# A transformer step with an expert loop: combination inside the next gate products, rows gathered in column tiles, second modulation on the gathered columns

## The reference

```
x = ln_affine(alpha * x + g1 * mix, ln1_g, ln1_b)
h = ln_plain(x) * (1 + sc2) + sh2                # sc2, sh2: one row for context, one for latent tokens
aff = softmax(h @ w_router)                      # 16 experts
gate, idx = top_k(aff.T, cap)                    # 16 of the 128 context tokens, 32 of the 256 latent ones per expert
hid = silu(h[idx] @ w_gate) * (h[idx] @ w_up)    # 1024 -> 2816, per expert
ye = (hid @ w_down) * gate                       # 2816 -> 1024
x = ln_affine(alpha * x + g2 * sum of ye at idx, ln2_g, ln2_b)
```

## Time and profile before

| | |
|---|---|
| median of three runs | 1884.5 us |
| profiled execution | 1881.69 us |
| its span, first to last instruction | 1879.9 us |
| mean granted share of TensorE's clock | 0.939 |
| PE busy | 1751.5 us (93%) |
| VectorE busy | 497.9 us (26%) |
| ScalarE busy | 296.9 us (16%) |
| GpSimd busy | 55.1 us (3%) |
| moved by DMA | 641.58 MB |
| gate and up products (L1096) | 673.3 us |
| down products (L1123) | 328.4 us |

### The profile page before, as it was taken

One profiled execution on the slowest core, in us unless ns is written; L12 is line 12 of the kernel. 1 busy time (PEld: TensorE's weight loads), 2 busy tenths in 40 slices (PEclk: granted clock), 3 DMA queues, 4 the chain that ended last, 5 costly groups with the idle time before them and its releaser, 6 DMA issues.

```text
span 1879.9 us, 19789 instructions
## 1 busy us (share of the span) xinstructions
PE 1751.5 (93%) x8298; PEld 888.3 (47%) x8298; DVE 497.9 (26%) x952; ACT 296.9 (16%) x633; POOL 55.1 (3%) x75
## 2 busy tenths in 40 slices
PE   5999999999979998999989999998999999999996
PEld 2767777778855343333443434333343433334332
DVE  5475647775670101010010101101010110101102
ACT  2443354453330000000000000000000000000000
POOL 2000000010030000000000000000000000000000
PEclk8999999999977999999989898988999999999998
DMA  9683243226565999999999999999999999999993
GB/s 357 226 285 88 96 126 93 84 90 236 223 243 243 423 404 426 430 430 430 434 428 432 429 430 430 429 432 427 416 424 423 414 432 430 429 430 431 431 432 153
DMA packets 60396, 641.58 MB, mean 341 GB/s; under 512 B 6093, under 2 KB 6237, under 8 KB 32701
## 3 DMA queue, kind: packets, MB, share of 16 engines
q1 hardware_dynamic: 56464, 629.96, 81.2%
q0 software_dynamic: 3888, 11.01, 1.8%
HBM read 637.25 MB, written 3.70 MB: 341 GB/s over the span
## 4 chain that ended last, share of the span: by engine, by line
PE 89%; DVE 6%; issue 2%; DMA 2%; ACT 1%; POOL 0%; SPq 0%; DVEq 0%; ACTq 0%
PE banks L1096 36%; PE banks L1123 17%; PE banks L771 16%; PE banks L1043 5%; PE banks L1131 4%; PE banks L769 2%; PE banks L1107 1%; PE banks L725 1%; DVE O L1880 1%; PE banks L786 1%; DMA ring<-in_w_in 1%; PE banks L927 1%; DVE O L1885 1%; PE banks L883 1%; PE banks L948 1%
## 5 line engine op out<-in xcount | busy, mean ns | idle before, releaser
L1096 PE MATMUL banks<-ring,O 128*64 128x512 f32 (+1 forms) x3072 | 673.3, 600 | 10.4 <-DVE O L1868 10.2
L1096 PEld LDWEIGHTS banks<-ring,O 128*64 128x64 f32 x3072 | 222.0, 141 | 451.6 <-issue 450.6
L1123 PE MATMUL banks<-ring,O 128*64 128x512 f32 x1408 | 328.4, 628 | 9.4 <-ACT O L1406 9.4
L1123 PEld LDWEIGHTS banks<-ring,O 128*64 128x64 f32 x1408 | 103.3, 145 | 225.5 <-issue 211.6
L1880 DVE TENSOR_TENSOR O<-O,banks 128x512 f32<-128x512 f32 (+1 forms) x48 | 28.0, 639 | 642.8 <-PE banks L1096 642.8
L771 PE MATMUL banks<-slot_parts,X_parts 128*128 128x512 f32 x672 | 184.8, 405 | 0.0
L771 PEld LDWEIGHTS banks<-slot_parts,X_parts 128*128 128x128 f32 x672 | 122.3, 190 | 39.9 <-issue 11.8
L1885 DVE TENSOR_TENSOR O<-banks,O 128x512 f32<-128x512 f32 x32 | 20.6, 686 | 376.1 <-PE banks L1123 376.1
L1546 DVE TENSOR_TENSOR slot_parts<-ring,slot_parts 128x512 fp32r<-128x512 f32 x168 | 105.2, 685 | 14.9 <-ACT slot_parts L1171 14.2
L1131 PE MATMUL banks<-O 128*128 128x512 f32 x192 | 86.2, 598 | 23.8 <-DVE O L1885 23.8
L1043 PEld LDWEIGHTS banks<-O 128*128 128x128 f32 x768 | 101.9, 216 | 8.5 <-issue 7.2
(11 more groups left out here) (265 smaller groups left out, 1071.2 us busy)
## 6 DMA issues: line engine op xcount, KB each, us to landing
ring<-in_w_exp_up SPq DMA_DIRECT2D x64, 2816.0 KB, 19.3
ring<-in_w_exp_gate SPq DMA_DIRECT2D x64, 2816.0 KB, 23.3
ring<-in_w_exp_down SPq DMA_DIRECT2D x32, 3072.0 KB, 16.8
...
ring<-in_w_mod SPq DMA_DIRECT2D x16, 1024.0 KB, 9.9
ring<-in_w_exp_down SPq DMA_DIRECT2D x16, 1024.0 KB, 22.1
O<-in_w_mod SPq DMA_DIRECT2D x8, 1024.0 KB, 5.2
```

The source lines that it names most:

```text
L1096: x = pe.matmul(banks[64 * w:64 * w + 64, 3 * m + b, 0:(i1 - i0) * P], xeT[:, k, :], w4[:, kk, w, i0 * P:i1 * P], start=(k == 0), stop=(k ...
L1123: x = pe.matmul(banks[64 * w:64 * w + 64, 6 + dc, :], hidT[:, i, 64 * w:64 * w + 64], wd[:, i, w, dc * BANK:(dc + 1) * BANK], start=(i == ...
```

## The change

Five things are changed.

1. The combination of expert e-1 moves into the gate products of expert e: three products after the first quarter, three after the second, into banks 3 to 5; VectorE's six adds move with it, to the start of its part of expert e. The combination of the last expert stays where it was. The slot broadcast of expert 0 moves from behind its gate products to behind their second quarter.
2. The rows of expert e+1 are gathered during expert e, between the turning of the hidden rows and the down products. The selection is now stationary (32 columns) and h2 moving (512 columns); the results of the two tile kinds and the two halves of D go to four groups of 32 partitions of one bank. ScalarE copies them, PE turns them (turn_expert, behind the first down group), and VectorE multiplies by 1 + sc2 and adds sh2 while it writes xeT.
3. h2 holds the plain normalised rows. GpSimd's and VectorE's modulation goes. The router weights are multiplied by 1 + sc2 beforehand (wrg), and 24 products add the share of sh2 to the logits (shift_logits). The order on ScalarE and VectorE around the norms changes with that, and tile 0 is normalised half by VectorE, half by ScalarE. The broadcasts of sc2 and sh2 become six small loads.
4. Feature 22 n + 2 i + w of the weights now lands in hidden column 128 i + n (before: 11 n + i), so gate and up products read elements 22 apart (before: 2) and the turning reads adjacent ones (before: 11 apart).
5. Within the last up quarter PE finishes block after block, VectorE gates each block when it is there, and each block is turned as soon as it is gated.

```diff
+        sc2k, sc2n, sh2k, sh2n = (O3[:, 2944 + 16 * i:2960 + 16 * i].rearrange("p (g k) -> p g k", g=2) for i in range(4))
+        sc2x, sh2x = (O3[:, 3008 + 16 * i:3024 + 16 * i].rearrange("p (i w g) -> p i w g", i=4, w=2) for i in range(2))
+        sc2x_m, sh2x_m = (x.rearrange("p i w g -> p (i w) g") for x in (sc2x, sh2x))
...
-        hid_cols = hid.rearrange("p (n i) -> p i n", i=FT)
-        h2_cols = O4[:].rearrange("p (t k n) -> p t k n", t=T, k=KT)
+        hid_cols = hid.rearrange("p (i n) -> p i n", i=FT)
         def h2_half(t, w):
-            return h2_cols[:, t, 4 * w:4 * w + 4, :]
-
-        def in_columns(row, w):
-            return row.rearrange("p (n k) -> p k n", k=KT)[:, 4 * w:4 * w + 4, :]
-
-        xeT = O3[:, BANK:2 * BANK].rearrange("p (k s) -> p k s", k=KT)
+            return h2[:, t, :].rearrange("p (n w k) -> p n w k", w=2, k=4)[:, :, w, :]
+        xe = O3[:, 0:BANK]
+        xe_cols = xe.rearrange("p (n k) -> p k n", k=4)
+        xeT = O3[:, BANK:2 * BANK].rearrange("p (m s) -> p m s", m=KT)
+        xeT_g = O3[:, BANK:2 * BANK].rearrange("p (m g s) -> p m g s", m=KT, g=2)
...
+            pool.dma_start(l1g, ln1_g.to_broadcast((P, D))).then_inc(bc_loaded, 16)
+            pool.dma_start(l1b, ln1_b.to_broadcast((P, D))).then_inc(bc_loaded, 16)
             for g in range(2):
                 pool.dma_start(g1b[:, g, :], mods[g, 2:3].to_broadcast((P, D))).then_inc(bc_loaded, 16)
-                pool.dma_start(sc2b[:, g, :], mods[g, 4:5].to_broadcast((P, D))).then_inc(bc_loaded, 16)
-            pool.dma_start(l1g, ln1_g.to_broadcast((P, D))).then_inc(bc_loaded, 16)
-            pool.dma_start(wr, w_router[0].rearrange("(p k) e -> p k e", p=P)).then_inc(bc_loaded, 16)
+            pool.dma_start(wr, w_router[0].rearrange("(k p) e -> p k e", p=P)).then_inc(bc_loaded, 16)
             pool.dma_start(iota_r, k_r[1:2].to_broadcast((P, NT))).then_inc(bc_loaded, 16)
-            pool.wait_ge(job_done, J_PB[-1] + 1)
-            for g in range(2):
-                pool.dma_start(sh2b[:, g, :], mods[g, 3:4].to_broadcast((P, D))).then_inc(bc_late, 16)
-            pool.dma_start(l1b, ln1_b.to_broadcast((P, D))).then_inc(bc_late, 16)
-            for n in range(2):
-                for w in range(2):
-                    dst = h2_half(t, w)
-                    pool.tensor_tensor(dst, dst, in_columns(sc2b[:, g, :], w), ALU.mult).then_inc(h2_scaled, 1)
-                    pool.wait_ge(h2_scaled, 2 * n + w + 1)
-                    pool.tensor_tensor(dst, dst, in_columns(sh2b[:, g, :], w), ALU.add).then_inc(h2_ready[n], 1)
+            for q, near, far in ((4, sc2k, sc2n), (3, sh2k, sh2n)):
+                pool.dma_start(near, mods[:, q].rearrange("g (p k) -> p g k", k=KT)).then_inc(bc_loaded, 16)
+                for g in range(2):
+                    pool.dma_start(far[:, g, :], mods[g, q].rearrange("(k p) -> p k", p=P)).then_inc(bc_loaded, 16)
...
+            def shift_logits(n):
+                t = ORDER[n]
+                for k in range(KT):
+                    pe.matmul(banks[:, 4 + t, 0:NE], sh2n[:, min(t, 1), k:k + 1].to_broadcast((P, P)), wr[:, k, :],
+                              start=(k == 0), stop=False)
             def logits(n, b):
                 t = ORDER[n]
                 pe.wait_ge(tb_out[b], F_H2[0] // 2 + n + 1)
                 for k in range(4 * b, 4 * b + 4):
-                    x = pe.matmul(banks[:, 4 + t, 0:NE], h2T[:, k, t * P:(t + 1) * P], wr[:, k, :],
-                                  start=(k == 0), stop=(k == KT - 1))
+                    x = pe.matmul(banks[:, 4 + t, 0:NE], h2T[:, k, t * P:(t + 1) * P], wrg[:, min(t, 1), k, :],
+                                  start=False, stop=(k == KT - 1))
                 if b:
                     x.then_inc(rt_log, 1)
...
-            pe.wait_ge(h2_ready[0], 2)
-            turn_tile(h2, 0)
+            pe.wait_ge(mod2_cols, 2)
+            for n in range(T):
+                shift_logits(n)
+            for n in range(2):
+                pe.wait_ge(h2_norm, n + 1)
+                turn_tile(h2, n)
+                for b in range(2):
+                    logits(n, b)
+            turn_probs(0)
+            pe.wait_ge(h2_first, 1)
+            turn_half(h2, 2, 0)
+            pe.wait_ge(h2_norm, 3)
+            turn_half(h2, 2, 1)
+            turn_probs(1)
             for b in range(2):
-                logits(0, b)
-            for n in (1, 2):
-                for b in range(2):
-                    pe.wait_ge(h2_ready[n], b + 1)
-                    turn_half(h2, n, b)
-                    if n == 2 and b:
-                        turn_probs(0)
-                    logits(n, b)
-            turn_probs(1)
+                logits(2, b)
             turn_probs(2)
...
-            def gather(k, ts):
-
-                s0 = k % 4 * SLOT + (LAT0 if ts[0] else CTX0)
+            def gather(ts):
                 for t in ts:
-                    x = pe.matmul(banks[:, 6 + k // 4, s0:s0 + CAP_L], h2_cols[:, t, k, :], sel[:, t, :],
-                                  start=(t == ts[0]), stop=(t == ts[-1]))
+                    s0 = LAT0 if t else CTX0
+                    for w in range(2):
+                        x = pe.matmul(banks[64 * w + s0:64 * w + s0 + CAP_L, 3, :], sel[:, t, :], h2_half(t, w),
+                                      start=(t < 2), stop=(t != 1))
                 return x
+            def turn_expert(n):
+                pe.wait_ge(xe_cp, n)
+                for i in range(4):
+                    x = pe.transpose(banks[:, 4, i * P:(i + 1) * P], xe_cols[:, i, :], ident)
+                x.then_inc(xet_done, 1)
...
-            for k in range(KT):
-                gather(k, (1, 2))
+            gather((1, 2))
...
-            for k in range(KT):
-                x = gather(k, (0,))
-            x.then_inc(xet_done, 1)
+            gather((0,)).then_inc(xe_done, 1)
+            turn_expert(1)
...
+            def combine(e, ns):
+                for n in ns:
+                    t, dc = divmod(n, 2)
+                    if n >= 3:
+                        pe.wait_ge(acc_done, e * 6 + (6 + n - 2))
+                    pe.matmul(banks[:, 3 + n % 3, :], selT[:, t * P:(t + 1) * P], yrow[:, dc * BANK:(dc + 1) * BANK],
+                              start=True, stop=True).then_inc(comb_done, 1)
+            def block_products(m, q, kk, b):
+                w4 = reg(((4 * m + q) % 6) * QUARTER, QUARTER).rearrange("p (k n i w) -> p k w i n", k=2, i=FT, w=2)
+                k = 2 * q + kk
+                i0, i1 = FCH[b]
+                for w in range(2):
+                    x = pe.matmul(banks[64 * w:64 * w + 64, 3 * m + b, 0:(i1 - i0) * P].rearrange("p (i n) -> p i n", n=P),
+                                  xeT[:, 2 * (k % 4) + k // 4, :], w4[:, kk, w, i0:i1, :], start=(k == 0), stop=(k == KT - 1))
+                return x
             def expert(e, first=False, last=False):
-                pe.wait_ge(xet_cp, 2 * e + 2)
+                pe.wait_ge(xet_cp, e + 1)
+                for q in range(4):
+                    pe.wait_ge(land_g[q], e * 16 + 16)
+                    for kk in range(2):
+                        for b in range(len(FCH)):
+                            x = block_products(0, q, kk, b)
+                    x.then_inc(gate_used, 1)
+                    if first:
+                        if q == 1:
+                            broadcast_slots()
+                    elif q == 0:
+                        pe.wait_ge(selT_ready, e)
+                        pe.wait_ge(y_cp, e * 2)
+                        combine(e - 1, range(3))
+                    elif q == 1:
+                        combine(e - 1, range(3, 6))
+                if first:
+                    pe.wait_ge(rt_cols, 2)
                 pe.wait_ge(acc_done, e * 6 + 6)
-
-                for m, (land, used) in enumerate(((land_g, gate_used), (land_u, up_used))):
-                    for q in range(4):
-                        pe.wait_ge(land[q], e * 16 + 16)
-                        w4 = reg(((4 * m + q) % 6) * QUARTER, QUARTER).rearrange("p (k m w) -> p k w m", k=2, w=2)
-                        for kk in range(2):
-                            k = 2 * q + kk
-                            for b, (i0, i1) in enumerate(FCH):
-                                for w in range(2):
-                                    x = pe.matmul(banks[64 * w:64 * w + 64, 3 * m + b, 0:(i1 - i0) * P],
-                                                  xeT[:, k, :],
-                                                  w4[:, kk, w, i0 * P:i1 * P], start=(k == 0), stop=(k == KT - 1))
-                        x.then_inc(used, 1)
-                    if first and m == 0:
-                        broadcast_slots()
-                        pe.wait_ge(rt_cols, 2)
-
-                pe.wait_ge(hid_done, e * 3 + 3)
+                for q in range(3):
+                    pe.wait_ge(land_u[q], e * 16 + 16)
+                    for kk in range(2):
```

(66 more changed lines are left out.)

96 lines of the change are left out of this document (44 added, 52 removed).

## The result

The changed kernel takes 2712.16 us (median of four runs, 2709.92 to 2714.87), the kernel before 1882.76 in the same comparison: ratio 1.438, 95% interval 1.429 to 1.448. The forecast was 1865, the range 1854 to 1880, and the rival that came true, (a), had 0.20 and a price of 2383 at its high end. The measured time lies beyond even that.

What follows compares the result with a forecast made beforehand. DMA and PE were taken as level, with DMA the bound after the change at 80.4 us per expert. Start -1, queue -9 and end -6.5 sum to -16.5; 1881.7 - 16.5 = 1865 us, range 1854 to 1880, leaving out (a).

Steps and rivals of the forecast that it cites:

- (a): Rival, every gate and up product: the wide step slows them, PE bounds the loop; up to 2383 us; chance 0.20.
- The weights read with a wide step: Gate and up products reading 22 elements apart: expected to cost nothing up to 15% on 41.4 us per expert.
- the low end: Gate and up products: wide step costs nothing, as 0.61 ns per element hides under 0.87 ns per column.
- The high end: Gate and up products: 1.70 ns per element, none hidden, 41.4 becoming 80.9 us; 111.8 per expert, 2383 us in all.
- The decision point of rival (a): Gate and up products: from 49.5 us for both, an expert takes PE more than the 80.4 us of transfers.
- PE in the loop: Expert loop: PE's work falls to 72.3 us per expert, gather 2.6 of it, against 80.4 us of transfers.
- The stretch before the loop: Norms, router and first gather before expert 0: sum -1 us, first gate product at 575, first maximum search at 556.2.
- The shift products: PE after the last output product: 48 records, 5.3 us at full clock or 10.1 at half; 5.3 taken.
- rival (b): Before the loop: shift products at half clock (+4.8) or gathers not abreast (+5); 1870 to 1875 us; chance 0.12.
- rival (c): Before the loop: shorter chain, VectorE no longer slowed beside GpSimd or clock staying high; 1858 us; chance 0.20.
- VectorE's wait for ScalarE: Before the loop: VectorE waits some 8 us for ScalarE's deviation of the second tile, until 541.6 instead of 533.3.
- The queue and the end: Loads at 430 GB/s, last landing 1264.4 us after first gate product: -9; products end 4.7 behind it: -6.5.

Runs made afterwards that it cites:

- experiment 4: Kernel of experiment 3 with the eight gate and up quarters read at steps 1, 2, 3, 4, 6, 8, 11, 22; not the layer; 2182.76 us.
- experiment 3: The full change but with the old feature order (weights 2 apart, turning 11 apart, waiting for all three blocks): 1868.88 us, ratio 0.990; repeated, 1865.24 us, ratio 0.992.
- experiments 7: Kernel of experiment 4 with two-dimensional patterns at steps 2 and 11, steps 12, 16, 32, and other groupings at 22; not the layer; 2387.07 us.
- 8: Kernel of experiment 4 with the eight quarters read at steps 14, 18, 20, 24, 26, 28, 30 and 44; not the layer; 2459.59 us.
- 9b: Kernel of experiment 3 with ScalarE's square roots ahead of tile 0's copies and VectorE's maxima behind tile 2's second norm: 1859.38 us, ratio 0.988.
- 9c: Kernel of 9b with VectorE summing the shift beforehand (3 products for 24) and tile 0's copies ahead of tile 2's square root: 1856.81 us, ratio 0.987.
- experiment 9a: Kernel of experiment 3 with each expert's combination back behind its down products, in six banks, adds behind the scaling: 1868.82 us, ratio 0.991.

## Why the prediction was wrong, and where it was right

**The weights read with a wide step: wrong.** I took the low end, nothing, "as 0.61 hides under 0.87", with up to 15% on it; it was 150%. The 0.61 was the difference of two stationary loads, as if a fetch were an addition to the product's pace. The curve of experiment 4 fits a pace of its own, of which the slower counts: 0.86 ns per column for the product, 1.75 for a fetch that serves one column. The row that I set aside had it: 218 ns for 128 elements 11 apart is 1.70 each, and products 11 apart measured 1.75 in experiment 4. The 3% at step 2, which I held against the rival, is no evidence for wide steps: there the fetch costs 0.88 per column and just disappears, it is at its limit. The argument that "the products already read two streams with gaps" used a row from below the bend to judge beyond it.

**The high end: too low as well.** 80.9 us for gate and up at 1.70; they took 103.5, since a step of 22 costs 2.3 ns. None of the rows that I bounded it by has that step, and experiments 7 and 8 show that of the even sizes tried only 20, 22 and 24 pay much more than the plateau. With 103.5 in place of 80.9, rival (a)'s sum gives 30.9 + 103.5 = 134.4 per expert, 2745 us; 28.6 for the rest instead of 30.9 makes it 2708.

**The decision point of rival (a), 49.5 us for both, was right and near.** It is 1.10 ns per column (49.5 over eight quarters of 5632), between step 2 and step 3. Nothing wider than 2 elements was affordable.

**A rule cited and set aside.** Steps 1 and 2 run at about full pace (2 costs 6% over 1), 3 costs 47% over 2, and from 4 on it is 94%. The Trainium skill (SBUF — State Buffer, Specifications) asks for two hits per 16-byte line, and the curve agrees; I cited it and gave it 0.20. The same page (Door 1: The DMA port swizzle) puts the free stride for fp32 at 4 elements; for this moving operand the measurement decides against that.

**PE in the loop without the step: right.** 72.3 us forecast, 70 to 72 busy in experiment 3; experts 80.4 apart forecast, 80.45 measured; waits for DMA at gate, up and down products as named. The gather took 1.84 us, four abreast, not the 2.6 of two abreast. The stationary loads of the turning went from 218 to 140 ns in the changed kernel, so part 4 does what it is for; that is 11 x 0.08 = 0.9 us per expert against 62.

**The stretch before the loop: right in sum.** 575 forecast, 574.81 in experiment 3 (575.20 when repeated), with the first maximum search at 555.60 where 556.2 was walked. In the changed kernel itself it is 578.25, because there the last output products end 4 us later (535.90 against 531.96). The shift products took 6.0 to 7.1 us, not 5.3: in the changed kernel some 36 of their 48 records fit into the first 4 us (535.9 to 539.9), at a granted clock of 0.96, and then the clock stood at 0.50. So the pace at full clock was right, and rival (b)'s half clock came for the last part. Of rival (c), VectorE's affine pass took 1.29 us where it took 2.54 beside GpSimd; the stretch didn't get shorter by it, since VectorE waited for ScalarE. VectorE's wait for ScalarE came as walked, some 8 us, and was longer, here in the changed kernel's timeline:

```profile
535.90 6.90 PE L994 MATMUL banks<-O 128*128 128x16 f32 x48
...
545.50 0.17 DVE L1503 RECIPROCAL sm<-sm 128x1 f32<-128x1 f32 x1 [11.25 <-ACT sm L1411]
```

Experiments 9b and 9c show that this wait and these products were worth 8 us of time.

**The queue and the end: right in experiment 3.** SyncE's queue, the last load, and its landing (us from the start of its issue) answer to the earlier trace rows; the last down products answer to the earlier trace rows:

```profile
1805.91 0.33 SPq L590 DMA_DIRECT2D ring<-in_w_exp_down  x1
```

```profile
ring<-in_w_exp_down SPq DMA_DIRECT2D x1, 1024.0 KB, 34.4
```

```profile
1831.47 13.95 PE L1166 MATMUL banks<-ring,O 128*64 128x512 f32 x64
```

1805.91 + 34.4 = 1840.3, which is 1265.5 us after the first gate product; forecast 1264.4 (its 8.4 MB and 15 x 34.6 MB at 430 GB/s make 1226.5 us and not 1225.8, so 1265.1). The products end at 1845.4, 5.1 behind it, forecast 4.7. But the cause lies elsewhere than in the combination: experiment 9a leaves it where it was and keeps the gain. What PE saved in the gather and in the waits must then have been enough to keep the queue full; no run takes these one by one.

**The clock.** The granted share went from 0.939 to 0.990 in the changed kernel and to 0.978 in experiment 3. In neither does it explain the time: in the stretch shown above PE has the full clock and still takes 132.1 us, and where six records of expert 0 ran at half the granted clock, 608 to 611 us, their starts were 1.17 to 1.20 us apart, as at full.
